# Stick-breaking attention in three single-rate passes instead of one plain fp32 matmul, with the mask in the scores and the early heads kept in HBM

## The reference

```python
z = jnp.einsum('bqhd,bkhd->bhqk', qb, k) * scale
causal = (s_pos[None, :] < t[:, None])
log_beta = jax.nn.log_sigmoid(z)
log_keep = jnp.where(causal, jax.nn.log_sigmoid(-z), 0.0)
after = lax.cumsum(log_keep, axis=3, reverse=True) - log_keep
a = jnp.where(causal, jnp.exp(log_beta + after), 0.0)
return jnp.einsum('bhqk,bkhd->bqhd', a, v)
```

## Time and profile before

| what | value |
|---|---|
| median of 3 runs | 2708.41 us (2706.26 to 2708.72) |
| span of the profiled execution | 2708.1 us, 26723 instructions |
| PE busy | 2523.3 us, 93% |
| VectorE, ScalarE, GpSimd busy | 1191.6, 587.6, 188.3 us |
| stick-breaking stage | from 931.5 to 1250.2 us of the span |

### The profile page before, as it was taken

How to read it: one execution, slowest core, us unless ns; L and a number is a source line. 1 busy time by engine, 2 the same in 40 slices (tenths; PEclk the granted TensorE clock), 3 DMA queues, 4 the chain that set the end, 5 groups by cost and what they waited for, 6 DMA issues and landing times.

```text
span 2708.1 us, 26723 instructions
## 1 busy us (share of the span) xinstructions
PE 2523.3 (93%) x10972; PEld 1977.1 (73%) x10972; DVE 1191.6 (44%) x1198; ACT 587.6 (22%) x697; POOL 188.3 (7%) x145
## 2 busy tenths in 40 slices
PE   5059999999999999988999999999999999999998
PEld 4048888888887655545666688887878888888887
DVE  5044444444444566545653243334354444444443
ACT  3021111111112344443423331112231111111111
POOL 1010000000000244431000000000200000000000
PEclk8579999999999999988998899999999999999999
DMA  9931111111111200001010011112111111111112
GB/s 141 33 56 47 47 46 46 46 51 57 47 46 45 103 16 16 16 8 31 32 38 1 1 55 55 54 48 101 62 40 53 48 46 46 46 53 48 46 46 70
DMA packets 48320, 128.01 MB, mean 47 GB/s; under 512 B 4059, under 2 KB 21979, under 8 KB 47707
## 3 DMA queue, kind: packets, MB, share of 16 engines
q1 hardware_dynamic: 45660, 113.15, 13.2%
q10 hardware_dynamic: 2592, 13.89, 5.6%
HBM read 115.10 MB, written 11.93 MB: 47 GB/s over the span
## 4 chain that ended last, share of the span: by engine, by line
PE 87%; DVE 5%; another core or an unknown queue 4%; ACT 2%; issue 1%; DMA 1%; SPq 0%; ACTq 0%; DVEq 0%
PE ps L1062 85%; PE ps L1373 1%; DVE h_lo L692 1%; DMA x_back<-x_keep 0%; DVE w_lo L685 0%; ACT pr_x L473 0%; ACT pr_x L475 0%; DVE pr_x L797 0%; DVE xT L740 0%; PE ps L1320 0%; DVE d_qk L805 0%; DVE d_qk L800 0%; DMA m_nat<-in_mem 0%; ACT pr_x L477 0%
## 5 line engine op out<-in xcount | busy, mean ns | idle before, releaser
L1062 PE MATMUL ps<-h_hi,w_hi 128*128 128x512 f32 x2240 | 887.9, 396 | 13.1 <-DVE h_lo L692 3.8
L1062 PE MATMUL ps<-h_lo,w_hi 128*128 128x512 f32 x2240 | 876.1, 391 | 0.0
L1062 PE MATMUL ps<-h_hi,w_lo 128*128 128x512 f32 x2240 | 692.9, 391 | 0.0
L1062 PEld LDWEIGHTS ps<-h_hi,w_hi 128*128 128x128 f32 x2240 | 422.8, 189 | 125.8 <-issue 33.0
L1062 PEld LDWEIGHTS ps<-h_hi,w_lo 128*128 128x128 f32 x2240 | 422.6, 189 | 89.4
L1062 PEld LDWEIGHTS ps<-h_lo,w_hi 128*128 128x128 f32 x2240 | 422.9, 189 | 86.9 <-issue 2.2
L413 ACT ACTIVATE w_hi<-raw 128x1024 fp32r<-128x1024 f32 x196 | 204.1, 1051 | 903.3 <-PE ps L1062 786.6
L685 DVE TENSOR_TENSOR w_lo<-raw,w_hi 128x1024 fp32r<-128x1024 f32 x196 | 254.5, 1306 | 271.4 <-ACT w_hi L413 260.4
L740 DVE TENSOR_TENSOR xT<-xT,ps 128x1024 f32<-128x1024 f32 x176 | 214.4, 1218 | 180.4 <-PE ps L1062 180.4
L1062 PE MATMUL ps<-a_hi,w_hi 128*128 128x512 f32 x704 | 275.7, 392 | 5.6 <-DVE w_lo L685 4.9
L1062 PE MATMUL ps<-a_lo,w_hi 128*128 128x512 f32 x704 | 274.6, 390 | 0.0
(11 more groups left out here) (172 smaller groups left out, 2046.0 us busy)
## 6 DMA issues: line engine op xcount, KB each, us to landing
raw<-in_weights SPq DMA_DIRECT2D x196, 512.0 KB, 3.5
x_nat<-in_x SPq DMA_DIRECT2D x8, 512.0 KB, 7.5
x_keep<-xT ACTq DMA_DIRECT2D x1, 4096.0 KB, 12.2
x_back<-x_keep ACTq DMA_DIRECT2D x1, 4096.0 KB, 13.5
out<-y_nat SPq DMA_DIRECT2D x8, 512.0 KB, 3.2
toe_keep<-toe ACTq DMA_DIRECT2D x2, 1728.0 KB, 100.4
m_nat<-in_mem SPq DMA_DIRECT2D x1, 1024.0 KB, 6.8
bias<-toe_keep ACTq DMA_DIRECT2D x2, 512.0 KB, 3.5
```

The lines of the kernel that those rows point to most:

```text
L1062: return pe.matmul(o, a, b, start=start, stop=stop, skip_group_check=True)
```

## The change

- `sb_q`, `sb_k`, `sb_v` are split in `q_hi`, `q_lo`, `k_hi`, `k_lo`, `v_hi`, `v_lo` (ACT makes the first of each pair in the new `proj_hi`, DVE the second in `proj_final`). The weights go to `a_all`, then DVE's new `sb_split_a` makes `sa_hi` (cast) and `sa_lo` (subtraction). Scores and values are three passes each. `sa_lo` lies where `a_all` does, one buffer where `sb_a` had two.
- The mask: one fp32r matmul behind the scores; the plain one behind the sums and DVE's multiplication by `causal` go.
- POOL's copy and add become one add that is 128 columns wider, with a memset once per head.
- `sb_sums_hi(s)` now stands behind `sb_softplus(s)` and `sb_split_a(s - 1)` in DVE's order.
- The values fill 128 rows of PSUM instead of 64. The second pair of q, k, v tiles and the second v take room; so only one slice of `o_sb` is held, and heads 0 to 3 go to HBM (`o_keep`) and come back in step 38, in three DMAs on ACT's queue.

```diff
@@ DVE
-                nc.vector.tensor_tensor(sb_l[:, s % 2, a:a + P], sb_l[:, s % 2, a:a + P], causal,
-                                        ALU.mult).then_inc(sb_sp_ready, 1)
-                dve.wait_ge(sb_sp_ready, s + 1)
...
+            def sb_split_a(s):
+                a = (7 - s % 8) * P
+                dve.wait_ge(sb_a_ready, s + 1)
+                nc.vector.tensor_copy(sa_hi[:, a:], a_all[:, a:]).then_inc(sb_a_hi, 1)
+                dve.wait_ge(sb_a_hi, s + 1)
+                nc.vector.tensor_tensor(sa_lo[:, a:], a_all[:, a:], sa_hi[:, a:].bitcast(F32),
+                                        ALU.subtract).then_inc(sb_a_split, 1)
...
+                if head in (2, 4):
+                    dve.wait_ge(o_kept, 8 * head)
+                nc.vector.tensor_copy(o_sb[r:r + HD, 2, :], ps[r:r + HD, 2, :]).then_inc(sb_o, 1)
...
+                sb_softplus(s)
+                if s:
+                    sb_split_a(s - 1)
                 sb_sums_hi(s)
-                sb_softplus(s)
@@ POOL
-                nc.gpsimd.tensor_copy(sb_sum[:, a:b], sb_l[:, s % 2, a:b]).then_inc(sb_sum_ready, 1)
-                if j < 7:
-                    nc.gpsimd.tensor_tensor(sb_sum[:, b:], sb_sum[:, b:], sb_l[:, s % 2, b:],
+                if j == 7:
+                    nc.gpsimd.memset(sb_sum[:, 0:a], 0.0).then_inc(sb_sum_ready, 1)
+                pool.wait_ge(sb_soft, s + 1)
+                if j == 7:
+                    nc.gpsimd.tensor_copy(sb_sum[:, a:], sb_l[:, s % 2, a:]).then_inc(sb_sum_ready, 1)
+                else:
+                    nc.gpsimd.tensor_tensor(sb_sum[:, a:], sb_sum[:, a:], sb_l[:, s % 2, a:],
                                             ALU.add).then_inc(sb_sum_ready, 1)
@@ ACT
+            def proj_hi(n):
+                h, i = divmod(n - PR_SB, 3)
+                if i < 2:
+                    act.wait_ge(pr_copied, n + 1)
+                    nc.scalar.activation((q_hi, k_hi)[i][h % 2][:], proj_dest(n)[:], ACT.Copy).then_inc(qk_hi_done, 1)
+                else:
+                    act.wait_ge(pr_aux, aux_before(n) + 1)
+                    nc.scalar.activation(v_hi[h % 2][:].rearrange("p b c -> p (b c)"), ps[:, aux_pair(n), :],
+                                         ACT.Copy).then_inc(v_hi_done, 1)
...
+                after(act, sb_av, s)
+                nc.scalar.activation(a_all[:, a:], ps[:, s % 2, a:], ACT.Exp).then_inc(sb_a_ready, 1)
...
+                if s in (19, 35):
+                    pair = s // 16 - 1
+                    act.wait_ge(sb_o, 2 * pair + 2)
+                    act.dma_start(o_keep[pair], o_sb[:, 2, :]).then_inc(o_kept, 16)
+                if s == 38:
+                    act.wait_ge(sb_av, 32)
+                    act.wait_ge(o_kept, 32)
+                    act.dma_start(o_sb[:, 0:2, :], o_keep.rearrange("h p s -> p h s")).then_inc(o_back, 16)
@@ PE
-                    last = mm(ps[:, s % 2, c:d], sb_k[r:r + HD, buf, j * P:(j + 1) * P], sb_q[r:r + HD, buf, c:d], True, False)
-                last.then_inc(sb_z, 1)
+                    mm(to, k_hi[buf][r:r + HD, key], q_hi[buf][r:r + HD, c:d], True, False)
+                    mm(to, k_hi[buf][r:r + HD, key], q_lo[buf][r:r + HD, c:d], False, False)
+                    mm(to, k_lo[buf][r:r + HD, key], q_hi[buf][r:r + HD, c:d], False, False)
+                mm(ps[:, s % 2, j * P:(j + 1) * P], mask_r[:, 0, :], mask_r[:, 1, :], False, False).then_inc(sb_z, 1)
...
-                mm(ps[:, s % 2, j * P:(j + 1) * P], ident, neg_mask, False, True).then_inc(sb_cum, 1)
...
-                pe.wait_ge(sb_a_ready, s + 1)
+                pe.wait_ge(sb_a_split, s + 1)
...
+                    mm(to, v_hi[buf][:, j, :], sa_hi[:, c:d], first, False)
+                    mm(to, v_hi[buf][:, j, :], sa_lo[:, c:d], False, False)
+                    last = mm(to, v_lo[buf][:, j, :], sa_hi[:, c:d], False, j == 0)
```

More of the change, by code:

```diff
@@ L160, in layer @@
         cst = at("cst", MISC, [P, 7, P])
-        ident, _, _, ones, head_ones, causal, neg_mask = (cst[:, i, :] for i in range(7))
+        ident, _, _, ones, head_ones, _, neg_mask = (cst[:, i, :] for i in range(7))
         mkT = at("mkT", MISC + 3584, [P, 2, MEM])
@@ L202, in layer @@
         o_x = at("o_x", AR + 16 * K, [P, 2, S])
-        sb_q = at("sb_q", AR + 24 * K, [P, 2, S])
-        sb_k = at("sb_k", AR + 32 * K, [P, 2, S])
-        sb_v = at("sb_v", AR + 40 * K, [P, 2, 8, P])
+        PAIR = (AR + 24 * K, AR + 48 * K)
+        q_hi = [at(f"q_hi{h}", PAIR[h], [P, S], F32R) for h in range(2)]
+        q_lo = [at(f"q_lo{h}", PAIR[h] + 4 * K, [P, S], F32R) for h in range(2)]
+        q_all = [at(f"q_all{h}", PAIR[h] + 4 * K, [P, S]) for h in range(2)]
+        k_hi = [at(f"k_hi{h}", PAIR[h] + 8 * K, [P, S], F32R) for h in range(2)]
+        k_lo = [at(f"k_lo{h}", PAIR[h] + 12 * K, [P, S], F32R) for h in range(2)]
+        k_all = [at(f"k_all{h}", PAIR[h] + 12 * K, [P, S]) for h in range(2)]
+        V_AT = (AR + 40 * K, AR)
+        v_hi = [at(f"v_hi{h}", V_AT[h], [P, 8, P], F32R) for h in range(2)]
+        v_lo = [at(f"v_lo{h}", V_AT[h] + 4 * K, [P, 8, P], F32R) for h in range(2)]
         sb_l = at("sb_l", XT, [P, 2, S])
@@ L211, in layer @@
         sp_lo = at("sp_lo", XT + 16 * K, [P, 2, S], F32R)
+        a_all = at("a_all", XT + 24 * K, [P, S])
+        sa_lo = at("sa_lo", XT + 24 * K, [P, S], F32R)
+        sa_hi = at("sa_hi", XT + 28 * K, [P, S], F32R)
         sb_sum = at("sb_sum", AR + 12 * K, [P, S])
@@ L321, in sum_count @@
             head, i = divmod(s, 8)
-            return head * 13 + (1 + 2 * i if i < 7 else 13)
+            return head * 8 + min(i + 2, 8)
         def sums_before(s):
@@ L563, in sb_weights @@
                 act.wait_ge(sb_cum, s + 1)
-                after(act, sb_av, s - 1)
-                nc.scalar.activation(sb_a[:, s % 2, a:], ps[:, s % 2, a:], ACT.Exp).then_inc(sb_a_ready, 1)
-            projections(PR_SB, PR_BESIDE)
+                after(act, sb_av, s)
+                nc.scalar.activation(a_all[:, a:], ps[:, s % 2, a:], ACT.Exp).then_inc(sb_a_ready, 1)
+            for n in range(PR_SB, PR_BESIDE):
+                split_hi(proj_unit(n) + AHEAD)
+                if n > PR_SB:
+                    proj_hi(n - 1)
+            proj_hi(PR_BESIDE - 1)
             act.wait_ge(x_kept, 16)
@@ L580, in _ @@
                     sb_weights(s - 1)
-                if square_of is not None:
+                if square_of is not None and square_of < PR_QX:
+                    proj_hi(square_of)
+                elif square_of is not None:
                     proj_rstd(square_of)
+                if s in (19, 35):
[6 more added lines that the diff above has]
+                    act.dma_start(o_sb[:, 0:2, :], o_keep.rearrange("h p s -> p h s")).then_inc(o_back, 16)
             def x_exp(n):
@@ L1258, in sb_cumulate @@
                     for c, d in bank_pieces(j * P, S):
-                        mm(ps[:, s % 2, c:d], tri_ones[:, 0, :], half[:, s % 2, c:d], False, False)
-                mm(ps[:, s % 2, j * P:(j + 1) * P], ident, neg_mask, False, True).then_inc(sb_cum, 1)
+                        last = mm(ps[:, s % 2, c:d], tri_ones[:, 0, :], half[:, s % 2, c:d], False, half is sp_lo)
+                last.then_inc(sb_cum, 1)
             def sb_values(s):
                 head, j = s // 8, 7 - s % 8
-                r, buf = (head % 2) * HD, (head // 2) % 2
-                pe.wait_ge(sb_a_ready, s + 1)
+                buf = (head // 2) % 2
+                pe.wait_ge(sb_a_split, s + 1)
                 if j == 7:
@@ L1490, in constants @@
     one = np.ones((P, P))
-    tiles = [i == j, -1.0 * (i >= j), -one, one, i // HD == j // HD, i < j, NEG * (i >= j)]
+    tiles = [i == j, -1.0 * (i >= j), -one, one, i // HD == j // HD, i == j, NEG * (i >= j)]
     return np.ascontiguousarray(np.stack([np.asarray(t, np.float32) for t in tiles], axis=1))
```

52 lines of the change are left out of this document (32 added, 20 removed).

## The result

The changed kernel takes 2734.09 us (median of 4 runs, 2731.75 to 2735.26) against 2708.0 for the kernel before on the same chip (median of 4, 2706.26 to 2708.72): a ratio of 1.0097, interval [1.0083, 1.0112]. It is slower by 26 us. The profiled execution spans 2732.7 us, 24.6 more than before.

A forecast was written before the change was run, and what follows sets the result against it. PE set the stage's pace before; now VectorE and GpSimd in one line: 242 + 44 + 25 waits + 16 gaps + 10 additions + 8 clock = 345 us, +26. With +2 at the start, 2708.1 becomes 2736 us; own range 2718 to 2755, overall 2702 to 2768.

The forecast's parts named there:

- the line: Stick-breaking stage: VectorE's and GpSimd's instructions run one after another and set the pace; stage 345 us against 318.7.
- the seven parts: Each step's sequence `sp_hi`, `sp_lo`, `sa_hi`, `sa_lo`, `sum_hi`, `sum_lo`, add: 242 us in the stage, 8.5 at 1024 columns.
- Waits: VectorE waits at each head's end for the weights (2.6 us) and the values (1.5): 25 us over six heads.
- Scores beside the line: PE's part in the line is only the sums and values at a head's end; scores add nothing to it.
- The clock: PE's granted clock in the stage: half of the up to 16 us lost before, so 8 us added.
- The rule that I weighed: VectorE's SBUF subtractions, multiplications or casts and any GpSimd work exclude each other; if casts did not, 62 us could overlap.
- Now `sum_hi` waits at the end of VectorE's step: `sum_hi` behind both splits stops `sum_lo` running beside the softplus addition, putting VectorE and GpSimd in one line.
- PE gets lighter, 43 us: PE in the stage: scores save 14.3 us, values 13.0, mask 5.3, plain-to-fp32r switches 10.6; a PE-bound stage would take 276.
- The small terms: Outside the line: start +2 us; memset, `o_sb` DMAs and splits of q and k 0; memset and DMAs up to 16.
- The add hides: Rival, chance 0.15: GpSimd's add runs beside casts and subtractions, 53 us leave the line; time 2710, no change.
- PE is the bound: Rival, chance 0.12: light matmuls give 43 us and VectorE keeps up; stage 276, time 2667.
- The clock falls: Rival, chance 0.15: PE idles in wide steps, half its sums and values run at half clock, 26 us more: 2762.

The follow-up runs named there:

- scores_only: Changed kernel with plain fp32 values and weights, no weights' split, two weight buffers and `sum_hi` first again; split scores and mask stay: 2704.95 us.
- hi_only: Changed kernel with ScalarE writing the weights directly as `sa_hi`; `sa_lo`, its values pass and VectorE's weights' split left out: 2698.98 us.
- cast_twice: Changed kernel with VectorE's cast of the weights to `sa_hi` issued a second time: 2755.91 us.
- all_vector: Changed kernel with all of GpSimd's work in the stage done by VectorE in the same places of the step: 2739.23 us.
- pe_pass: Changed kernel with a fourth pass, `k_lo` by `q_lo`, added to the scores: 2746.37 us.
- sums_early: Changed kernel with the cast `sum_hi` back at the front of VectorE's step, ahead of softplus and weights' split: 2795.69 us.
- hi_vector: hi_only with GpSimd's stage work done by VectorE and `sum_hi` at the front of the step: 2681.86 us.

## Why the prediction was right, and where it was not

**The direction and the size** were right: 2736 forecast, 2734.1 measured; the stage 345 forecast, 341.7 measured. The core of the reason given, that the weights' split is put into VectorE's part of what each step must pass through, is borne out by `scores_only`, `hi_only` and `cast_twice`. That GpSimd's work stands in one line with it is borne out in part: the rows show the collisions and `all_vector` rules out the opposite, but the line is full for 281 of 342 us only, not for "nearly the whole stage". The wide step of 8.5 to 9 us came out: heads 0 to 2 have 8.6 us each at width 1024, with 1.5 to 2.6 us of waiting for the Ln in them that the seven parts did not have. Later heads, with more beside them, take 9.3 to 13.3. Of my signs, PE waits for `sum_lo` (24 times, 16.7 us) and `sum_hi` follows right behind `sa_lo`; but `sp_hi` is hardly stretched in five of six heads at 1024 columns, which is close to what I had named as a sign of being wrong.

**The composition was not.** I summed 296 us of work in the line (242 + 44 + 10) and 49 us of gaps, waits and clock. The trace has at least one of the two engines busy for 281 us and both idle for 60. The two errors, 15 too much and 11 too little, nearly cancel; that the forecast lies within 2 us of the measurement is luck. Three terms were mis-sized:
- *Waits.* I gave VectorE 25 us at the heads' ends. There it waits for the weights and the values for 34.1 (23.6 + 10.5). The 78 us for ScalarE's Ln are in no term; a part lies beside GpSimd's subtraction, the rest is the round through PE's scores.
- *"Scores beside the line".* By `pe_pass`, 12.4 us more in the scores cost 12.3. They are in the round.
- *The clock.* I took 8 us on top of the line. The granted clock fell from 0.95 to 0.90 on average: from 0.97 to 0.95 in heads 0 to 3, and from 0.90 to 0.84 in heads 4 and 5 (1127.71 to 1245.94 us before, 1139.55 to 1267.53 after). How much of the loss of heads 4 and 5 (9.8 us) is the clock, and how much the query norms of VectorE that stand there in collision with GpSimd, no run here separates.

The rule that I weighed, that a subtraction or a cast of VectorE and any work of GpSimd exclude each other, is too wide by one case. Beside GpSimd's subtractions and adds it holds in the rows shown here: 2.89 us for a `sp_lo` of 1.09, 2.02 for a cast of 0.23. Beside its memset, which reads nothing, VectorE's subtraction kept its 0.29 us:

```profile
1135.89 0.84 POOL L412 MEMSET sb_sum<- 128x896 f32 x1
...
1135.95 0.29 DVE L949 TENSOR_TENSOR sp_lo<-sb_l,sp_hi 128x128 fp32r<-128x128 f32 x1
```

The Trainium skill, "SBUF — State Buffer", section "SBUF: two separate sides", states it so: a VectorE instruction in a two-port mode excludes GpSimd's, one with two SBUF inputs only a GpSimd instruction that reads SBUF. By it the casts were exclusive, and the traces agree; the prediction left out the condition, which changes nothing in its sum.

**"Now `sum_hi` waits at the end of VectorE's step"** was named as a cause, and is a cure. `sums_early` costs 62 us more. This is the step of the reasoning that failed: I looked for what the move takes from GpSimd's overlap and not for what it frees. With the split in the step, `sum_hi` in front waits for PE's last sums, and pushes the add onto `sp_lo`.

**"PE gets lighter, 43 us"** was too high. The switch between 64 and 128 rows adds 0.10 to the first pass of the scores and 0.09 to the last, the mask takes 0.17 instead of 0.12, and the pass behind it 0.28 instead of 0.23: 0.3 us a step, 14 in the stage, more than the 10.6 credited for the plain-to-fp32r switches that went away. That leaves a relief of some 29 us. By the columns about 8.5 of them lie in the four narrow steps (an estimate from the prediction's terms), 1.4 a head, and the time there fell by 0.7 a head. `scores_only`, with the scores' share alone, gains 3 us.

**The small terms.** Start: +2 forecast, +1.6 measured. The memset: 0 forecast; it takes 0.84 us, begins when `sum_lo` is done, and stands in no wait of the stage. The DMAs of `o_keep` appear in no wait of the stage. The splits of q and k, 0 forecast: in VectorE's groups of the stage `q_lo` takes 2.6 us in the mean and `k_lo` 1.8 where 1.22 would do. The two `k_lo` stand in narrow steps, whose times did not grow; the two `q_lo` stand in the steps of 768 columns of heads 0 and 2, which took 0.4 us more and 0.2 less than before. The end of the stage I had only inside the six head-end waits: its 3.0 us are the last split and its passes, in the timeline's last rows. PE had idled for 3.10 us, and two passes of 512 columns stand 0.42 us apart there, not 0.23; the granted clock from 1270.5 to 1273.5 us is 0.50, that is 1.2 GHz instead of 2.4:

```profile
1269.32 1.23 DVE L958 TENSOR_TENSOR sa_lo<-a_all,sa_hi 128x1024 fp32r<-128x1024 f32 x1
...
1270.59 0.79 PE L1122 MATMUL ps<-sa_hi,v_hi 128*128 128x512 f32 x1 [3.10 <-DVE sa_lo L958]
...
1272.04 0.63 PE L1122 MATMUL ps<-sa_hi,v_hi 128*128 128x512 f32 x1
...
1272.46 0.63 PE L1122 MATMUL ps<-sa_lo,v_hi 128*128 128x512 f32 x1
...
1273.56 1.23 DVE L975 COPY o_sb<-ps 64x1024 f32<-64x1024 f32 x1 [0.63 <-PE ps L1122]
```

**The rivals.** *The add hides* (2710): half of it did. It runs beside the softplus addition (1.22 of 2.13 us in the rows above), but not beside the casts. *PE is the bound* (2667): no; PE idles for 52 us. Even `hi_vector`, with one pass less and GpSimd gone, comes only to 2682. *The clock falls* (2762): it fell by 0.05 on average, mainly in the last heads; what that cost is not measured, but the time did not come out at 2762.

What stays open: the share of the clock, in heads 4 and 5 above all and in the costs of the experiments; how much of GpSimd's work lies in VectorE's waits; and what makes PE idle 6 us longer in `scores_only`, which takes back most of its 10 us of lighter work.
